# Weight splits of the fourth mixer on GpSimd, and the order of score products and shades in the second and third

## The reference, cut to what matters

```
s = q @ k.T (two products summed in the second mixer), scaled
s = where(mask, s, -inf)        # mask_mla, mask_da, mask_sw
p = softmax(s)                  # the third mixer subtracts two such maps, the fourth adds a sink
o = p @ v
```

## Time and profile before

| | |
|---|---|
| median of 3 runs | 1379.5 us |
| lowest and highest | 1372.33 and 1381.71 us |
| profiled execution, first to last instruction | 1371.8 us |
| device time of the profiled execution itself | not listed apart from these runs |
| PE busy | 1339.3 us (98%) |
| DVE busy | 891.0 us (65%) |
| ACT busy | 710.5 us (52%) |
| POOL busy | 193.4 us (14%) |
| mean granted clock of PE | 0.995 |

### The profile page before, as it was taken

How to read it: one execution, slowest core, us unless ns; L and a number is a source line. 1 busy time by engine, 2 the same in 40 slices (tenths; PEclk the granted TensorE clock), 3 DMA queues, 4 the chain that set the end, 5 groups by cost and what they waited for, 6 DMA issues and landing times.

```text
span 1371.8 us, 18975 instructions
## 1 busy us (share of the span) xinstructions
PE 1339.3 (98%) x7229; PEld 1135.7 (83%) x7229; DVE 891.0 (65%) x1539; ACT 710.5 (52%) x1209; POOL 193.4 (14%) x342
## 2 busy tenths in 40 slices
PE   9999998899999999999999999999999999999998
PEld 8899897778888888888888887888888877888887
DVE  6886887567555467475554699875554587755553
ACT  7765464335444356464443566654443566544441
POOL 2386888500200000000000000000000000000000
PEclk9999999999999999999999999999999999999999
DMA  9666655436555546265555455065555431565552
GB/s 263 192 157 159 141 167 161 108 124 200 185 185 190 181 139 196 78 185 185 186 190 189 139 191 173 23 214 184 184 184 194 159 123 62 170 199 185 187 191 82
DMA packets 172163, 226.46 MB, mean 165 GB/s; under 512 B 11832, under 2 KB 137594, under 8 KB 172074
## 3 DMA queue, kind: packets, MB, share of 16 engines
q1 hardware_dynamic: 166976, 213.03, 48.8%
q0 software_dynamic: 3328, 10.24, 3.5%
q10 hardware_dynamic: 1770, 1.99, 0.5%
HBM read 219.77 MB, written 5.45 MB: 164 GB/s over the span
## 4 chain that ended last, share of the span: by engine, by line
PE 70%; POOL 11%; DVE 9%; DMA 4%; issue 3%; ACT 2%; SPq 0%; POOLq 0%; DVEq 0%; ACTq 0%
PE psum L961 21%; PE psum L963 21%; PE psum L962 21%; POOL vectors L3285 5%; POOL vectors L3288 4%; DVE w_low L708 2%; DMA ring<-in_gdn_w_in 2%; PE psum L1435 1%; PE psum L1395 1%; PE psum L1468 1%; PE psum L952 1%; DVE work L880 1%; PE psum L1194 1%; DMA consts<-keys_scratch 1%; PE psum L1454 1%
## 5 line engine op out<-in xcount | busy, mean ns | idle before, releaser
L708 DVE TENSOR_TENSOR w_low<-ring,w_high 128x1024 fp32r<-128x1024 f32 (+3 forms) x395 | 476.6, 1217 | 320.1 <-ACT w_high L694 319.6
L694 ACT ACTIVATE w_high<-ring 128x1024 fp32r<-128x1024 f32 (+3 forms) x395 | 410.7, 1048 | 423.8 <-PE psum L963 405.5
L961 PE MATMUL psum<-w_high,hT 128*128 128x512 f32 (+2 forms) x944 | 371.2, 393 | 0.0
L963 PE MATMUL psum<-w_high,hT 128*128 128x512 f32 (+2 forms) x944 | 366.1, 388 | 0.0
L962 PE MATMUL psum<-w_low,hT 128*128 128x512 f32 (+2 forms) x944 | 365.5, 387 | 0.0
L961 PE MATMUL psum<-w_high,parts 128*128 128x512 f32 (+1 forms) x532 | 209.6, 394 | 1.1 <-DVE parts L2751 1.1
L963 PEld LDWEIGHTS psum<-w_high,hT 128*128 128x128 f32 x944 | 177.2, 188 | 36.5
L963 PE MATMUL psum<-w_high,parts 128*128 128x512 f32 (+1 forms) x532 | 206.7, 389 | 0.0
L962 PE MATMUL psum<-w_low,parts 128*128 128x512 f32 (+1 forms) x532 | 206.6, 388 | 0.0
L962 PEld LDWEIGHTS psum<-w_low,hT 128*128 128x128 f32 x944 | 177.5, 188 | 33.8
L961 PEld LDWEIGHTS psum<-w_high,hT 128*128 128x128 f32 x944 | 177.4, 188 | 33.7
(11 more groups left out here) (308 smaller groups left out, 1410.8 us busy)
## 6 DMA issues: line engine op xcount, KB each, us to landing
ring<-in_ffn_w_gate_up SPq DMA_DIRECT2D x176, 256.0 KB, 3.1
ring<-in_w_gate_up SPq DMA_DIRECT2D x176, 256.0 KB, 3.1
ring<-in_gdn_w_in SPq DMA_DIRECT2D x48, 512.0 KB, 5.5
ring<-in_ffn_w_down SPq DMA_DIRECT2D x44, 512.0 KB, 3.2
ring<-in_w_down SPq DMA_DIRECT2D x44, 512.0 KB, 3.2
ring<-in_da_w_qkv SPq DMA_DIRECT2D x24, 512.0 KB, 3.9
ring<-in_gdn_w_out SPq DMA_DIRECT2D x16, 512.0 KB, 3.8
ring<-in_mla_w_out SPq DMA_DIRECT2D x8, 512.0 KB, 4.1
```

Of the source, the lines that this page charges most:

```text
L694: nc.scalar.activation(piece_slot(w_high, n), piece_slot(ring, n), ACT.Copy).then_inc(s.w_hi, 1)
L708: nc.vector.tensor_tensor(piece_slot(w_low, n), piece_slot(ring, n), piece_slot(w_high, n).bitcast(F32), ALU.subtract).then_inc(s.w_lo, 1)
L961: mm(out, lhs[0], rhs[0], start=start, stop=False)
L963: return mm(out, lhs[1], rhs[0], start=False, stop=stop)
```

## The change

Two things change.

In the second and third mixers (`shades_last=True`, the default), `scores(i)` makes the products of both query tiles first, the second mixer all 128-row products and then all 64-row products, and after them all shades. Only the first product into a bank, that of tile 0, has the start flag; the last shade of tile 1 has the stop flag. The fourth mixer keeps the order that all had.

In the fourth mixer the four pieces that ScalarE and VectorE split during the rounds are split by GpSimd instead: a copy to the high part and a subtraction to the low part, one piece after the other, each as soon as its slot is free and the piece has landed. ScalarE and VectorE wait behind the rounds until the counts have come to the end of these pieces.

```diff
         a_sout = add_projection(a["sw_w_o"], 8)
+        POOL_SPLITS = range(a_sout.first - 4 + SPLIT, a_sout.first + SPLIT)
...
-        sw_rounds = Rounds(sem, "sw", SW_HEADS // 2, HD ** -0.5, (shade_window, shade_causal), HD, q_by)
+        sw_rounds = Rounds(sem, "sw", SW_HEADS // 2, HD ** -0.5, (shade_window, shade_causal), HD, q_by, shades_last=False)
...
+                def products(i, t, n):
+                    u = i % 2
+                    for j in range(2):
+                        mm(B[2 * u + j][:, keys_of(t)], q(i, j, t)[n], k(i, j, t)[n], start=(n == 0 and (t == 0 or not A.shades_last)),
+                           stop=False, skip_group_check=A.shades_last)
+                def shaded(i, t):
+                    u = i % 2
+                    for j in range(2):
+                        tiles_ = [(kt, A.masks[1 if kt == t else 0]) for kt in range(t + 1)]
+                        tiles_ = [(kt, shade) for kt, shade in tiles_ if shade is not None]
+                        for n, (kt, shade) in enumerate(tiles_):
+                            last = mm(B[2 * u + j][:, (t + kt) * P:(t + kt + 1) * P], ident_b, shade, start=False,
+                                      stop=(n == len(tiles_) - 1 and (t == T - 1 or not A.shades_last)), skip_group_check=A.shades_last)
+                    return last
...
+                    parts_ = range(len(q(i, 0, 0)))
+                    if A.shades_last:
+                        for n in parts_:
+                            for t in range(T):
+                                products(i, t, n)
+                        for t in range(T):
+                            last = shaded(i, t)
+                    else:
+                        for t in range(T):
+                            for n in parts_:
+                                products(i, t, n)
+                            last = shaded(i, t)
...
# ScalarE
-                elif 3 <= i < 7:
-                    split_high(act, a_kv + 5 + i + SPLIT)
             attention(sw_rounds, True, beside_round, last_squares)
             empty_banks(act, tp_so, 1)
+            act.wait_ge(s.w_hi, POOL_SPLITS.stop)
...
# VectorE
-                elif i < 5:
-                    split_low(dve, a_kv + 5 + i + SPLIT)
-                elif i > 5:
-                    split_low(dve, a_kv + 4 + i + SPLIT)
...
+            dve.wait_ge(s.w_lo, POOL_SPLITS.stop)
...
# GpSimd, at its end
+            for n in POOL_SPLITS:
+                pool.wait_ge(s.w_hi, n)
+                pool.wait_ge(w_ready[n % RING], landings(n))
+                pool.wait_ge(s.piece_used, n - SPLIT + 1)
+                copy(piece_slot(w_high, n), piece_slot(ring, n)).then_inc(s.w_hi, 1)
+                pool.wait_ge(s.w_hi, n + 1)
+                pool.wait_ge(s.w_lo, n)
+                tt(piece_slot(w_low, n), piece_slot(ring, n), piece_slot(w_high, n).bitcast(F32), ALU.subtract).then_inc(s.w_lo, 1)
```

More of the change, by code:

```diff
@@ L256, with __init__ @@
 class Rounds:
-    def __init__(self, sem, name, rounds, scale, masks, dv, by=None):
+    def __init__(self, sem, name, rounds, scale, masks, dv, by=None, shades_last=True):
         self.rounds, self.scale, self.masks, self.dv, self.by = rounds, scale, masks, dv, by
+        self.shades_last = shades_last
         self.scores = sem(f"{name}_scores")
@@ L1428, in round_scores @@
             def round_scores(A, q, k):
-                def scores(i):
[L1431 to L1441, removed]
+                def products(i, t, n):
[3 more added lines that the diff above has]
+                           stop=False, skip_group_check=A.shades_last)
```

## The result

The changed kernel takes 1380.16 us in the median (20 runs, 1377.15 to 1389.95), the kernel before on the same chip 1373.95 us (20 runs, 1371.55 to 1381.71). The ratio is 1.0048, with a 95% interval of 1.0033 to 1.0063: **6.6 us slower** (4.5 to 8.7), against the 8.9 that were forecast. The absolute forecast, 1388 us, is 7.8 above the measured median. Of this, 5.5 us are in the starting point (1379.5 was a median of three runs; twenty gave 1373.95) and 2.3 in the sum. The profiled execution of after spans 1378.6 us, 6.8 more than before. Seven of the 20 runs of after form a group of their own, 1387.6 to 1390.0 us at a mean granted clock of 0.984 or 0.985, while the traced execution is one of the other thirteen, 1377.2 to 1380.8 us at 0.991 to 0.995; what the seven spent their 8 us on was not traced.

What follows compares the result with a forecast made beforehand. TensorE, busy in 98% of the span, was taken to bound the kernel. Scores late 7.5, maxima 3.3, splits taken away -1.1 and shades last -0.8 gave +8.9 us on 1379.5: 1388 us, range 1374 to 1397.

Steps and rivals of the forecast that it cites:

- the emptying: Fourth mixer: VectorE empties a transposed bank, at 1120.39 before; PE's round 0 scores wait for it; forecast 6.5 us late.
- Direction and mechanism: Fourth mixer: VectorE and GpSimd block each other for whole instructions, so PE waits and the kernel gets slower, 1388 us, +0.64%.
- GpSimd's durations: Fourth mixer: a 128x1024 copy takes 1.1 us and a subtraction 2.3, so 3.4 a piece and 14 for four.
- Scores of round 0 late: Fourth mixer: VectorE's four multiplications wait for GpSimd, delaying PE's first scores 6.5 us, 8.7 with a third subtraction; 7.5 taken.
- Round 0's maxima: Fourth mixer: GpSimd's last piece delays the four short VectorE instructions that ScalarE's exponentials wait for, 3.3 us more.
- Taken away: Fourth mixer: without ScalarE's split ahead of round 7's exponentials, PE's transposes start earlier; 1.1 us less.
- All shades last: Second and third mixers: one return from full to half rows less per round, paying in seven rounds; 0.8 us less.
- The sum: Whole kernel: 7.5 + 3.3 - 1.1 - 0.8 = +8.9 us, added to the starting median.
- The starting point: Whole kernel before the change: median 1379.5 us, with the profiled execution, 1371.8 us, taken as about the quickest run.
- The queues slip past each other: Rival, fourth mixer: VectorE passes at GpSimd's seams or copies don't block; PE loses under 2 us, 1377.6 with nothing lost; chance 0.22.
- Much slower: Rival, fourth mixer: everything blocks at proportional GpSimd durations, cold clock on top; +16 less 1.9, 1393 to 1395 us; chance 0.15.
- Late pieces: Rival, fourth mixer: GpSimd needs over 8 us a piece and PE waits at the output projection; some 1395 us; chance 0.03.

Runs made afterwards that it cites:

- experiment 3: Changed kernel, but GpSimd only fills the four pieces' buffers with zeros and reads nothing: fourth stage 38.03 us, ratio 0.999 to the kernel before.
- experiment 4: Changed kernel, but GpSimd only fills 8 columns of each buffer, signals kept, splits left out: fourth stage 36.93 us, ratio 0.9985 to the kernel before.
- experiment 5: Changed kernel with each GpSimd copy and subtraction cut into four of 256 columns: fourth stage 42.37 us, ratio 1.0021 to the kernel before.
- experiment 6: Changed kernel, but GpSimd makes only the four high-part copies and VectorE the subtractions: fourth stage 38.03 us, ratio 0.9975 to the kernel before.
- experiment 1: Changed kernel with the GpSimd splits put back on ScalarE and VectorE, only the shades' order kept: fourth stage 38.21 us, ratio 0.9988 to before.
- experiment 7: Changed kernel, but GpSimd starts only after round 4's scores: fourth stage 48.31 us, ratio 1.007 to the kernel before.
- experiment 2: Changed kernel with the old order of scores and shades, only the GpSimd splits kept: fourth stage 45.96 us, ratio 1.0053 to the kernel before.

## Why the prediction was right or wrong, point by point

The direction, the place and the mechanism held. What failed is the step that follows the emptying: "GpSimd's last 3.4 us fall on round 0's maxima", put at 3.3 us. They fell behind these maxima, and 2.0 us of delay came there from the half clock instead. Beside it three sizes were off: the scores' delay (7.5 put, 5.8 measured), the gain of the shades (0.8 put, 1.5 measured) and the starting point (1379.5 put, 1373.95 measured).

- **Direction and mechanism: right.** Whole instructions of VectorE and GpSimd take turns, at exactly the place named, and PE waits for the emptying. Experiments 3, 4, 5 and 6 show it by four different GpSimd loads. The Trainium skill, SBUF — State Buffer, section "Who interferes with whom", has the rule, and the runs bear out its finer parts as well: a GpSimd instruction that only writes does not hinder a two-input one of VectorE (0.69, experiment 3) but does hinder a TENSOR_SCALAR from SBUF to SBUF, which the section counts among those that can take the shared pair (0.95 instead of 0.17), and a reduction and a copy with their input in PSUM were not hindered (1.02 and 0.68 beside a subtraction).
- **GpSimd's durations: right.** 1.04 and 2.39 us, against 1.1 and 2.3. The slope between the two short forms in the earlier trace rows held out to 1024 columns.
- **Scores of round 0 late: +7.5 put, +5.8 measured; the mis-sized term.** I reached 6.5 by adding four times 0.35 us own time to the waits, and then moved up to 7.5 for a third subtraction that could fall in. The own times lie mostly beside GpSimd's: the emptying starts 0.2 us behind the third copy, and from the first subtraction's end to the emptying it is 5.03 us, of which the next three of GpSimd's take 4.86 (1.23 + 2.40 + 1.23). Undisturbed, a copy takes 1.04, and the three would take 4.47, so the four multiplications add 0.6 us and not 1.4. The third subtraction came beside the emptying, which has its input in PSUM and did not wait; it held up only the TENSOR_SCALAR behind it, which nobody waited for. That own times are hidden was to be seen in the earlier trace rows: a pair of splits lost 0.35 us to an operation that needs at least 0.6.
- **Round 0's maxima: +3.3 put; the step that failed, as a cause, and +2.0 measured from another.** VectorE's four instructions behind round 0's maxima ran undisturbed at 0.16 to 0.17 us each, because GpSimd's fourth piece waited until PE had used its slot (1131.9, idle 3.90 us), and this was itself late. What made the first transposes 7.8 us late instead of 5.8 is the half clock: scores and the last query products took that much longer, and ScalarE's output of these products (1131.79, behind PE's L965) stands ahead of its exponentials. I had named the clock as coming in place of the maxima; it was the only one of the two. GpSimd's fourth subtraction then held up the first instruction behind round 1's maxima (L2544, 0.96 us), and round 1's values waited 0.52 us: from round 0's transposes to these values it is 7.05 us, where it was 6.31.
- **Taken away: -1.1 put, -1.3 measured** (experiment 4 against 1). Round 7's transposes start without the 0.71 us wait; of the 0.26 us between their halves 0.20 are left.
- **All shades last: -0.8 put, -1.5 measured; mis-sized.** I priced the return from full to half rows at 0.09 us by the shades' own durations. Measured is 0.26 us for a third-mixer round (1.40 to 1.14) and 0.36 for a second-mixer round (2.86 to 2.50): eight half-row products in one run take 0.86 us, two runs of four took 0.42 + 0.63 = 1.05. Most of the gain (0.19 of the 0.26) is in the products themselves, whose durations I had kept: I looked at what follows a run and not at what its beginning costs. That I counted only seven rounds was sound in kind: in the third mixer new waits of 0.25 us for VectorE appear, and of 0.26 per round only 0.7 in all arrives.
- **The sum.** By its steps: 5.8 + 2.0 + 0.7 (round 1) - 1.3 - 1.5 = 5.7, against 5.85 by the stages, where the forecast had 7.5 + 3.3 - 1.1 - 0.8 = 8.9. Both terms of loss were too large and the gain of the shades too small, all in the same direction; the 0.7 of round 1 stood nowhere in the forecast and made up for a part of it by luck.
- **The starting point: 1379.5 put, 1373.95 measured.** It is 5.5 of the 7.8 us by which the absolute figure missed. I compared the profiled span of 1371.8 us with whole device times and took the profiled execution for a quick one. In the runs beside the experiments an execution's device time is 1.9 us above its span (1374.18 against 1372.3), which makes 1373.7 for the profiled one, nearly the median of twenty. That 1% is about what a measurement can tell was wrong too: twenty runs gave an interval of 0.3%.
- **Slips in the working.** The new round adds to 1.29 us by the earlier trace rows, which have 0.63 and not 0.64, and 6.5 us with a third subtraction of 2.3 makes 8.8 and not 8.7; neither changes the sum.
- **Rivals.** "The queues slip past each other" is refuted by the emptying (5.8 us late, its point was 2). "Much slower" is refuted by the durations and by the clock's 2 us being all there is. "Late pieces": the last low part was done at 1135.4, the projection began at 1165.8.

## What to carry to other kernels

An idle GpSimd is no free engine beside a VectorE on the critical path: ask how many of its instructions VectorE's chain will meet there, since even an instruction on four elements a partition waited for a whole one (2.25 us in experiment 7). Give it short instructions (quarters cost 5.4 us here, whole ones 8.6) or a stretch in which VectorE reads PSUM or is not waited for; rounds full of short dependent VectorE instructions were the worst place tried. When a stall ends, count the clock behind it as well (2.0 us here). On TensorE, put products on half the rows in one run: it took 0.26 and 0.36 us off a round.

## What the runs showed of the hardware that I had not expected

- Splitting a subtraction of GpSimd's into quarters costs it 16% (2.78 against 2.39 us), and 40% (3.34) where VectorE takes its turns in between; it saves PE 3.2 us (42.37 against 45.55).
- Size is no protection and the operation decides: of two instructions of VectorE on 128x16 from SBUF to SBUF, both beside a subtraction, the RECIPROCAL took 0.25 us as before and the TENSOR_SCALAR 1.71 us in place of 0.16.
- The same 14 us of GpSimd work cost 8.6 us ahead of the rounds and 11.4 in the middle of them (48.31 - 36.93).
- The half clock lasted longer in experiment 2: there the last product in front of round 1's scores still took 0.63 us, in the changed kernel 0.40, and the fourth stage was 0.4 us longer for the same program in that stage.
